# A hybrid decoder layer on one core: the twelve matmuls of a block product ordered by partial product instead of by slice

## The reference

```python
x = half_swiglu(x, ffn1_norm, ffn1_w_gate, ffn1_w_up, ffn1_w_down)
h = rmsnorm(x, mix_norm);  proj = h @ w_in
# dilated window attention and RWKV-7 time mixing on proj
x = x + merged @ w_out
x = half_swiglu(x, ffn2_norm, ffn2_w_gate, ffn2_w_up, ffn2_w_down)

def half_swiglu(x, g, w_gate, w_up, w_down):
    h = rmsnorm(x, g)
    return x + 0.5 * ((silu(h @ w_gate) * (h @ w_up)) @ w_down)
```

## Time and profile before

| quantity | value |
|---|---|
| median of three runs | 1766.95 us |
| the profiled execution | 1768.82 us |
| its span, first to last instruction | 1767.0 us |
| TensorE matmul busy | 1696.9 us (96%) |
| VectorE, ScalarE, GpSimd busy | 941.4, 737.6, 698.1 us |
| mean granted TensorE clock | 0.983 of full |
| share of TensorE in the chain that ended last | 81% |
| of it, the block products (L824) | 23% |

### The profile page before, as it was taken

How to read it: one execution, slowest core, us unless ns; L and a number is a source line. 1 busy time by engine, 2 the same in 40 slices (tenths; PEclk the granted TensorE clock), 3 DMA queues, 4 the chain that set the end, 5 groups by cost and what they waited for, 6 DMA issues and landing times.

```text
span 1767.0 us, 41483 instructions
## 1 busy us (share of the span) xinstructions
PE 1696.9 (96%) x16580; PEld 1614.2 (91%) x16580; DVE 941.4 (53%) x1483; ACT 737.6 (42%) x1227; POOL 698.1 (40%) x912
## 2 busy tenths in 40 slices
PE   6799999999799999999999999999999699999998
PEld 6799999999799999898788989898999699999998
DVE  6736537366854545454474453626455744637363
ACT  4444536355523333332243443435234453536442
POOL 3564645554422222121132322324255463645543
PEclk9899999999899999999899999999999899999999
DMA  4352433423432334232054454446353352343522
GB/s 171 126 184 75 140 132 119 155 73 130 150 119 97 103 111 143 93 100 70 31 208 183 169 183 157 180 147 232 137 204 119 131 171 107 115 138 116 188 67 98
DMA packets 57497, 237.29 MB, mean 134 GB/s; under 512 B 7521, under 2 KB 8161, under 8 KB 55905
## 3 DMA queue, kind: packets, MB, share of 16 engines
q1 hardware_dynamic: 49440, 218.35, 34.8%
q10 hardware_dynamic: 7872, 16.37, 2.5%
HBM read 216.93 MB, written 71.76 MB: 163 GB/s over the span
## 4 chain that ended last, share of the span: by engine, by line
PE 81%; issue 6%; DVE 6%; POOL 3%; ACT 2%; DVEq 1%; DMA 0%; ACTq 0%; POOLq 0%
PE ps L394 27%; PE ps L824 23%; PE ps L834 14%; PE ps L1401 3%; POOL w_lo L381 3%; PE ps L2339 1%; PE ps L2516 1%; ACT w_hi L374 1%; PE ps L2453 1%; PE ps L2439 1%; PE ps L2383 1%; PE ps L2459 0%; PE ps L2423 0%; PE ps L1366 0%; PE ps L1521 0%
## 5 line engine op out<-in xcount | busy, mean ns | idle before, releaser
L381 POOL TENSOR_TENSOR w_lo<-w_raw,w_hi 128x256 fp32r<-128x256 f32 x384 | 320.1, 864 | 714.8 <-ACT w_hi L374 714.8
L394 PE MATMUL ps<-h_hi,w_hi 128*128 128x288 f32 x1248 | 295.2, 319 | 35.5 <-POOL w_lo L381 31.5
L394 PE MATMUL ps<-h_hi,w_lo 128*128 128x288 f32 x1248 | 270.5, 299 | 0.0
L394 PE MATMUL ps<-h_lo,w_hi 128*128 128x288 f32 x1248 | 270.4, 299 | 0.0
L394 PEld LDWEIGHTS ps<-h_hi,w_hi 128*128 128x128 f32 x1248 | 204.9, 193 | 57.6 <-POOL w_lo L381 33.1
L394 PEld LDWEIGHTS ps<-h_lo,w_hi 128*128 128x128 f32 x1248 | 204.8, 192 | 0.0
L394 PEld LDWEIGHTS ps<-h_hi,w_lo 128*128 128x128 f32 x1248 | 204.1, 192 | 0.0
L807 POOL TENSOR_TENSOR ring_lo<-raw,ring_hi 128x256 fp32r<-128x256 f32 (+1 forms) x194 | 140.5, 749 | 119.7 <-ACT ring_hi L788 118.9
L374 ACT ACTIVATE w_hi<-w_raw 128x1024 fp32r<-128x1024 f32 x96 | 101.7, 1059 | 110.7 <-PE ps L394 93.7
L1209 DVE SCALAR_TENSOR_TENSOR x<-ps,x 128x576 f32<-128x576 f32 x64 | 48.5, 758 | 145.5 <-PE ps L834 144.4
L807 POOL TENSOR_TENSOR ring_lo<-w_raw,ring_hi 128x256 fp32r<-128x256 f32 (+1 forms) x123 | 88.3, 743 | 79.9 <-ACT ring_hi L788 79.7
(11 more groups left out here) (447 smaller groups left out, 3958.1 us busy)
## 6 DMA issues: line engine op xcount, KB each, us to landing
w_raw<-in_w SPq DMA_DIRECT2D x122, 512.0 KB, 3.4
raw<-in_w SPq DMA_DIRECT2D x48, 512.0 KB, 4.8
kv<-in_kc SPq DMA_DIRECT2D x32, 576.0 KB, 5.8
kv<-in_vc SPq DMA_DIRECT2D x32, 576.0 KB, 7.0
cache_out<-in_cache SPq DMA_DIRECT2D x28, 576.0 KB
raw<-in_w_down SPq DMA_DIRECT2D x32, 384.0 KB, 3.7
w_raw<-in_w_down SPq DMA_DIRECT2D x16, 384.0 KB, 3.5
gates<-gate_out ACTq DMA_DIRECT2D x16, 288.0 KB, 2.4
```

Source lines behind the costliest of these rows:

```text
L381: last = nc.gpsimd.tensor_tensor(w_lo[par_][:, c], w_raw[par_][:, c], w_hi[par_][:, c].bitcast(F32), ALU.subtract)
L394: last = nc.tensor.matmul(ps[:, b + c, 0:HC], w[par_][:, wk], a[:, k, c * HC:(c + 1) * HC], start=(first and k == 0), stop=(end and k == n ...
```

## The change

In `product` the two loops are exchanged: the outer loop now goes over the three partial products and the inner one over the four slices. The wait for the block's low part moves from the front of the product to the front of the third partial product, which is the ninth matmul; in front stands a wait for the block's high part. The matmuls, their operands, their bank and the signal at the end are the same.

```diff
             b = (kind, v)
             i = AT[f][b]
-            block_ready(pe, f, b)
-            for k in range(4):
-                wk = slice(128 * k, 128 * k + 128)
-                for n, (w, r) in enumerate(((ring_hi, a_hi[a]), (ring_hi, a_lo[a]), (ring_lo, a_hi[a]))):
+            pe.wait_ge(hi_done, hi_count(f, i))
+            for n, (w, r) in enumerate(((ring_hi, a_hi[a]), (ring_hi, a_lo[a]), (ring_lo, a_hi[a]))):
+                if n == 2:
+                    block_ready(pe, f, b)
+                for k in range(4):
+                    wk = slice(128 * k, 128 * k + 128)
                     last = nc.tensor.matmul(ps[:, bank, 0:HC], w(f, i)[:, wk], r[:, k, :], start=(first and k == 0 and n == 0),
                                             stop=(k == 3 and n == 2), skip_group_check=True)
             last.then_inc(sem("blk_used"), 1)
```

## The result

The changed kernel takes 1773.58 us, the median of five runs (1771.70 to 1777.08), against 1766.95 us before. The ratio is 1.0038 with a 95% interval of 1.0024 to 1.0053: it is slower, by 6.6 us. The two series disagree on the size of the loss: 0.0022 is only 3.9 us. The forecast was 1767.0 us, with a range of 1763.2 to 1771.2 us.

A forecast was written before the change was run, and what follows sets the result against it. The prediction took TensorE, almost always running matmuls, to bound the kernel. Gaps, waits and order each added 0 to the profiled 1768.82 us, which gave 1767.0 us against a median of 1766.95 us; range 1763.2 to 1771.2 us.

The forecast's parts named there:

- What bounds the kernel: TensorE, busy 1696.9 of 1767.0 us; only its idle stretches or the distance between matmul starts can move the time.
- The moved wait at the gaps: Two idle gaps before the first `S2` product, 5.23 and 5.02 us, end at VectorE's chunk, not the low part; gain 0.
- The price of one more wait: One extra, already met wait in each of 259 block products; taken as 0, between -2.6 and +2.6 us.
- The sign that the twelve starts must be evenly spaced: Check within a block product: even starts would confirm the forecast, a longer distance to the ninth would show the mid-product wait costing.
- Rival 3: The wait in mid-product stalls the ninth matmul's load, about 6 us slower, 1773 us; chance 0.08.
- The order itself: Reordering 3108 block-product matmuls leaves 132.2 ns each; cost taken as 0, with bounds of 3.3 us either way.
- Rival 1: Block products slow to the down products' 133.3 ns as the high, low, high activation pattern ends; 1770.3 us, chance 0.17.
- rival 2: Block products quicken to 131.1 ns per matmul because reloading the same weights costs most; 1763.7 us, chance 0.17.
- Two equations for two unknowns: Down- and block-product rates solved for step costs: 134.4 ns with the same weights, 131.1 ns with different ones.
- The sum: Whole program: profiled 1768.82 us plus 0 for gaps, waits and order, giving 1767.0 us as the median.
- The rule against the change: One weight load can serve many matmuls, so separating a high slice's uses might lose; taken as nothing, since every matmul loads.

The follow-up runs named there:

- The two series: The changed kernel measured twice against the kernel before: five runs, ratio 1.0038, then twelve runs of the same kernel, ratio 1.0022.
- wait_only: Kernel before with its order by slice kept, high-part wait in front, low-part wait ahead of the third matmul; ratio 1.0009.
- order_only: Kernel before with the twelve matmuls ordered by partial product, low-part wait still in front of the product; ratio 1.0029.
- hi_lo_hi_weights: Kernel before, by slice, but each slice goes high by high, low weights by high activations, high weights by low activations; 132.2 ns per matmul.
- pairs_kept: Kernel before, but each slice does high by high then high by low, with the four low-weight matmuls at the end; 132.2 ns per matmul.
- all eight kernels with the later fall: The changed kernel and seven experiment kernels whose full clock lasted 358.4 us before falling, against 355.0 us in the kernel before.
- slices_0213: Changed kernel's order by partial product, but low-part wait in front and slices going 0, 2, 1, 3; 133.3 or 131.7 ns per matmul.

## Why the prediction was wrong, by its steps

**What bounds the kernel: right.** TensorE has no gap in the block products but the two, and what they lose is in the distance of their matmuls.

**The moved wait at the gaps: right.** They are 5.21 and 4.97 us (5.23 and 5.02 us before). VectorE's chunk (now L1195) again ends last in both layers, 0.1 us before TensorE starts at 88.97 and 1414.30 us.

**The price of one more wait: right at the value taken, and the bound was too wide.** 0 was taken, between -2.6 and +2.6 us. `wait_only` has 39 of them in a stretch of 61.88 us, which is as long as without. The sign that the twelve starts must be evenly spaced was badly chosen: they aren't in the kernel before either (127 to 139 ns). Rival 3, the mechanism that I had put on the slower side, did not act.

**The order itself: the step that failed.** The prediction gave three values, -3.3, 0 and +3.3 us, and took 0 because each of the outer two "needs a cause that no row shows alone". The change went to the upper one: 133.35 ns, 3.5 us. `order_only` has this rate without the moved wait, and `wait_only` the old one with a moved wait. The 0 for the order was the term that failed. Rival 1, at 0.17, had the rate right, for a reason that was wrong: it spoke of a high, a low and again the high activation slice together, and `hi_lo_hi_weights` and `pairs_kept` keep the lower rate without it. The row that bore on the choice was the down products': the same shape on the same engine at 133.3 ns. "The block products run at one rate over all operands and ring places" says nothing against a loss, since the order was the one thing that all of them had in common.

**The rate of the load that repeats: rival 2 fell.** After the change no two matmuls in a row load the same weights, and the step is not 131.1 ns. Two equations for two unknowns had fitted, as the prediction said they always would.

**The sum: a term was missing.** It treated all that lies outside the block products as fixed. The stages behind layer 1 start 1.5 us later, and where TensorE's clock falls in them moves against the work. One stretch of 37 us costs 0.7 to 1.0 us more in all eight kernels with the later fall. Of the 6.6 us of the first series, the rate has 3.5 us and this stretch 0.9 us. The cause of the other 2.2 us stays open: the profiled execution has 1.3 us more in the stretch 464 to 495 us, but also -4.2 and +3.6 us further on, and the second series, 3.9 us in all, has no room for them. Besides, the kernel before had been seen in three runs within 0.9 us, while 35 later runs spread over 7.3 us. The upper end, 1771.2 us, was rival 1 (1770.3) and less than 1 us for everything else. With half of this spread on top of 1770.3 us it should have stood near 1774 us.

**The rule against the change.** The prediction drew from the Trainium skill ("TensorE: Matmul & The Clock Gate", section "Step-by-step: what each phase is for") that putting two uses of the same weights apart might give something away. The change did become slower, but not by this: `hi_lo_hi_weights` puts them apart as well and loses nothing. The same page, in "Back-to-back issue gap", gives N / 2.4 + 2.5 ns for an isolated matmul (an estimate of 122.5 ns for 288 columns), and for a stream of pairs of a load and a matmul about 81 ns at 128 columns and 131 ns at 512. The streams here took 131.7 to 133.3 ns at 288 columns already, and in neither figure of the page is there a term for the order, which is up to 1.7 ns.

## What to carry to other kernels

Where TensorE is busy without a gap, the order of its matmuls within a product is not free, even if each has its own load: divide the length of a gapless stretch by its matmuls, for each order that the kernel already has, and take the rate of the stream whose order the new one resembles. A wait for a signal that came long ago cost nothing measurable in such a stream (at most 0.01 us for 39 of them). In a long program, a shift of 0.6 to 1.6 us put a fall of the clock off by 3.4 us, from a wait into the work behind it, and a stretch of 37 us took 0.7 to 1.0 us more. Another stretch gained or lost 1.2 to 1.5 us in the same way; leave room for that in a range, measure the same kernel in a second series, and compare profiles stretch by stretch before a difference of two totals is explained.

## What the runs showed of the hardware that was not expected

Matmuls of 288 columns at the full clock settled at 133.3, 132.5, 132.2 or 131.7 ns a step, by their order and, in one kernel, by nothing that the code changed: `slices_0213` ran at 133.3 ns in five groups of tiles and at 131.7 ns in three. Each pattern, once reached, held to the end of its gapless stream of up to 39 products. Why a stream keeps one of them is open.

These rates are means. Single steps lie between 127 and 139 ns and repeat: in the kernel before every product takes the same 12 x 132.2 ns, in the changed one the products take 133.7 and 133.0 ns per matmul in turn.

The clock was slow for 55 to 71 us of each of the seventeen profiles, in short stretches. Where they lie, and whether they fall on work or on a wait, makes the two largest differences between the profiles before and after: -4.2 us at 803 to 906 us and +3.6 us at 1298 to 1377 us.
